# A decoder layer with routed experts on one core: routing each token tile beside the out projection instead of after it

## The reference

```python
x = x + merged @ w_out[l]
h2 = rms_norm(x, norm2_g[l])
...
gl = hf @ w_gr + b_gr                      # 4 groups
g_idx = argmax(gl); p_g = softmax(gl)[g_idx]
el = hf @ w_er + b_er                      # 4 x 8 experts
top_v, top_i = top_k(el[g_idx], 2)
w = softmax(top_v) * p_g
# each token goes through its 2 experts: (silu(h w_gate) * (h w_up)) w_down, weighted by w and added to x
```

## Time and profile before

| | us |
|---|---|
| median of 3 runs (lowest, highest) | 1543.49 (1543.43, 1547.29) |
| the profiled execution, its own time | 1544.72 |
| its span, first to last instruction | 1542.8 |
| TensorE busy in the span | 1428.2 (93%) |
| VectorE, ScalarE, GpSimd busy | 987.5, 790.1, 380.5 |
| mean granted TensorE clock | 0.965 of full speed |

### The profile page before, as it was taken

One profiled execution on the slowest core, in us unless ns is written; L12 is line 12 of the kernel. 1 busy time (PEld: TensorE's weight loads), 2 busy tenths in 40 slices (PEclk: granted clock), 3 DMA queues, 4 the chain that ended last, 5 costly groups with the idle time before them and its releaser, 6 DMA issues.

```text
span 1542.8 us, 20443 instructions
## 1 busy us (share of the span) xinstructions
PE 1428.2 (93%) x7251; PEld 1204.1 (78%) x7252; DVE 987.5 (64%) x1333; ACT 790.1 (51%) x1090; POOL 380.5 (25%) x497
## 2 busy tenths in 40 slices
PE   4899999999999999999999928999999999999980
PEld 4788888888888788888888827888888888888860
DVE  5664664664674532434332275988998898998865
ACT  5553453453453322323221235778787888887750
POOL 5324424424434200000000011223323323222310
PEclk9999999999999999999999859999999999999995
DMA  5210210210210334433152318999999999999958
GB/s 161 59 42 1 59 42 1 59 42 1 59 42 1 82 90 115 137 103 103 41 189 109 133 44 294 373 379 387 383 382 383 390 384 386 386 379 380 383 211 329
DMA packets 132130, 290.18 MB, mean 188 GB/s; under 512 B 15968, under 2 KB 94944, under 8 KB 107488
## 3 DMA queue, kind: packets, MB, share of 16 engines
q1 hardware_dynamic: 121696, 268.31, 48.4%
q0 software_dynamic: 9216, 16.80, 3.0%
q10 hardware_dynamic: 1152, 4.19, 0.7%
HBM read 280.87 MB, written 25.17 MB: 198 GB/s over the span
## 4 chain that ended last, share of the span: by engine, by line
PE 88%; DVE 3%; DMA 2%; POOL 2%; ACT 1%; issue 1%; SPq 0%; POOLq 0%; DVEq 0%; ACTq 0%
PE proj L87 17%; PE proj L89 17%; PE proj L88 17%; PE scores L87 7%; PE scores L89 7%; PE scores L88 7%; PE scores L665 2%; PE outs L729 2%; PE scores L545 2%; DMA comb<-y_rows 1%; PE turned L87 1%; PE turned L89 1%; PE turned L88 1%; PE outs L806 1%; PE turned L545 1%
## 5 line engine op out<-in xcount | busy, mean ns | idle before, releaser
L1642 DVE TENSOR_TENSOR w_low<-w_slot,w_high 128x2048 fp32r<-128x2048 f32 x192 | 438.3, 2290 | 68.4 <-ACT w_high L1078 67.4
L1078 ACT ACTIVATE w_high<-w_slot 128x2048 fp32r<-128x2048 f32 x192 | 367.0, 1918 | 120.4 <-DMA w_slot<-in_w_gate 63.8
L87 PE MATMUL proj<-w_high,xeH 128*128 128x512 f32 x512 | 203.8, 398 | 3.1 <-DVE xeL L1663 3.1
L89 PE MATMUL proj<-w_high,xeL 128*128 128x512 f32 x512 | 200.9, 392 | 0.0
L88 PE MATMUL proj<-w_low,xeH 128*128 128x512 f32 x512 | 200.4, 391 | 0.0
L913 ACT ACTIVATE wCH<-wC_in 128x1024 fp32r<-128x1024 f32 x48 | 47.6, 1052 | 155.7 <-DMA wC_in<-in_w_branch_b 155.7
L1321 DVE TENSOR_TENSOR wCL<-wC_in,wCH 128x1024 fp32r<-128x1024 f32 x48 | 56.9, 1236 | 92.2 <-ACT wCH L913 92.2
L87 PEld LDWEIGHTS proj<-w_high,xeH 128*128 128x128 f32 x512 | 97.1, 190 | 23.1 <-DVE xeL L1663 2.8
L89 PEld LDWEIGHTS proj<-w_high,xeL 128*128 128x128 f32 x512 | 96.8, 189 | 21.0
L88 PEld LDWEIGHTS proj<-w_low,xeH 128*128 128x128 f32 x512 | 97.0, 189 | 19.5
L87 PE MATMUL proj<-wBH,hTH 128*128 128x512 f32 x256 | 111.5, 436 | 0.0
(11 more groups left out here) (283 smaller groups left out, 3139.8 us busy)
## 6 DMA issues: line engine op xcount, KB each, us to landing
w_slot<-in_w_gate SPq DMA_DIRECT2D x64, 1024.0 KB
w_slot<-in_w_up SPq DMA_DIRECT2D x64, 1024.0 KB, 8.4
w_slot<-in_w_down SPq DMA_DIRECT2D x64, 1024.0 KB, 8.3
wC_in<-in_w_in SPq DMA_DIRECT2D x32, 512.0 KB, 5.0
wB_in<-in_w_in SPq DMA_DIRECT2D x16, 512.0 KB, 6.3
comb<-y_rows SPq DMA_DIRECT2D x16, 512.0 KB, 9.8
wA_in<-in_w_in SPq DMA_DIRECT2D x12, 512.0 KB, 6.3
x_all<-in_x SPq DMA_DIRECT2D x4, 1024.0 KB, 8.1
```

Of the source, the lines that this page charges most:

```text
L87: pe.matmul(out, lh, rh, start=start, stop=False)
L89: return pe.matmul(out, ll, rh, start=False, stop=stop)
L1078: act.activation(w_high[c][:], w_in6[c][:], ACT.Copy).then_inc(S["gu_high" if c < 4 else "d_high"], 1)
L1642: dve.tensor_tensor(w_low[c][:], w_in6[c][:], w_high[c][:].bitcast(F32), ALU.subtract).then_inc(S["gu_low" if c < 4 else "d_low"], 1)
```

## The change

Routing is done tile by tile, in the out projection's own time:

- TensorE's order has one loop of 16 halves, cnt = 8n + i. Between the products of half cnt stand the transposes of the residual x2's half before it (turn_half, not normalised) and the router product of that half (route_half), accumulated over the two halves by VectorE. The router's weights are multiplied by norm2_g first (wrg, GpSimd, from a new load g2_cols of norm2_g by columns), and the logits of a tile by its rstd afterwards.
- VectorE does a tile's routing in the steps top_group, two_experts (MAX and MAX_INDEX give the two best of 32) and place_rows; TensorE makes the tile's positions (positions_of) and adds its token numbers into one bank (rows_of).
- ScalarE squares by halves, copies the turned halves and scales h2; GpSimd multiplies h2 by norm2_g. Slots 0 and 1 of the first expert are loaded after half 0 and their w_high and w_low made in tiles 1 and 2 of half 1; slot 2 is loaded after the last out product, slot 3 after the last store of h2, slots 4 and 5 after the first gather.
- GpSimd gathers the first three experts from ids_gather directly, without the copy. The first expert's rows are transposed, and their high and low parts made, in two halves; its gate product waits for the first half only.
- The routing weights (gexp, vexp, wsel) are made after the row numbers. Several semaphores are merged.

```diff
+            sp.dma_start(g2_cols[:], T["norm2_g"][0].rearrange("(k p) -> p k", p=P),
+                         allow_slow_non_contiguous=True).then_inc(S["router_in"], DMA)
...
+            load_gu(0, (0, 1))
...
             sp.wait_ge(S["d_done"], 16)
-            load_gu(0, (0, 1))
+            load_gu(0, (2,))
+            store_h2(N_TILES - 1)
+            load_gu(0, (3,))
+            sp.wait_ge(S["xe_landed"], DMA)
...
+            def turn_half(cnt):
...
+                pe.wait_ge(S["x2_done"], cnt + 1)
...
+                for j in range(4):
+                    last = pe.transpose(bank(cnt % 2)[:, j * 128:(j + 1) * 128],
+                                        x2[:, i, n * 512 + j * 128:n * 512 + (j + 1) * 128], ident)
+                last.then_inc(S["x2T_done"], 1)
+            def route_half(cnt):
...
+                if cnt == 0:
+                    pe.wait_ge(S["wrg_done"], 1)
+                pe.wait_ge(S["x2T_out"], cnt + 1)
+                if n == 1:
+                    pe.wait_ge(S["logit_done"], cnt - 7)
+                for j in range(4):
+                    last = pe.matmul(OB[:, 36 * i:36 * i + 36], x2T[:, cnt % 2, j, :], wrg[:, 4 * n + j, :],
+                                     start=(j == 0), stop=(j == 3))
+                last.then_inc(S["lg_done"], 1)
+            def positions_of(t):
+                if t == 0:
+                    pe.wait_ge(S["masks_out"], 1)
+                else:
+                    pe.wait_ge(S["place_step"], 3 * t - 2)
+                pe.wait_ge(S["before_done"], 2 * t + 1)
+                last = pe.matmul(bank(2)[:, 0:32], count_masks[:, 0:128], mask[:, t, :], start=True, stop=(t == 0))
+                if t:
+                    last = pe.matmul(bank(2)[:, 0:32], count_masks[:, 128:256], before[:, t, :], start=False, stop=True)
+                last.then_inc(S["pos_mm"], 1)
+            def rows_of(t):
+                pe.wait_ge(S["place_step"], 3 * t + 3)
+                for c in range(2):
+                    last = pe.matmul(bank(3)[:, 0:32], pick[:, t % 2, c, :], keyid1[:, t, c, :],
+                                     start=(t == 0 and c == 0), stop=(t == 7 and c == 1))
+                last.then_inc(S["rows_mm"], 1)
+            for cnt in range(16):
+                out_proj(cnt, range(0, 2))
+                if cnt >= 1:
+                    turn_half(cnt - 1)
+                out_proj(cnt, range(2, 5))
+                if cnt >= 1:
+                    route_half(cnt - 1)
+                if cnt >= 10:
+                    positions_of(cnt - 10)
+                out_proj(cnt, range(5, 8))
+                if cnt >= 11:
+                    rows_of(cnt - 11)
+            turn_half(15)
+            route_half(15)
+            positions_of(6)
+            rows_of(5)
+            positions_of(7)
+            rows_of(6)
+            rows_of(7)
...
+            for half, done in ((0, "x0_T"), (1, "xeT_done")):
+                for k in range(4 * half, 4 * half + 4):
+                    last = pe.transpose(SC[:, 0, k * 128:(k + 1) * 128], xe[:, DS(k, 128, step=8)], ident)
+                last.then_inc(S[done], 1)
+            for c in range(4):
+                pe.wait_ge(S["gu_low"], c + 1)
+                if c == 0:
+                    pe.wait_ge(S["x0_L"], 1)
+                if c == 2:
+                    pe.wait_ge(S["xeL_done"], 1)
+                gate_up(pe, c).then_inc(S["w_free_gu"], 1)
...
+            for cnt in range(16):
+                square_half(cnt)
+                turned_half(cnt)
...
+                if cnt in (9, 10):
+                    high(w_high[cnt - 9][:], w_in6[cnt - 9][:], S[f"w_land{cnt - 9}"], DMA, S["gu_high"])
+                if cnt >= 8:
+                    i = cnt - 8
+                    act.wait_ge(S["n2_rstd"], 2 * i + 3)
...
+                    act.activation(h2[:, i % 2, :], x2[:, i, :], ACT.Copy, scale=rstd2[:, i:i + 1]).then_inc(S["h2_scaled"], 1)
...
+            for c in (2, 3):
                 high_slot(c, DMA)
-            x_high(1)
+            act.wait_ge(S["route_step"], R_DIFFS)
+            act.activation(gexp[:], gdiff[:], ACT.Exp).then_inc(S["weight_exps"], 1)
+            act.activation(vexp[:], vdiff[:], ACT.Exp).then_inc(S["weight_exps"], 1)
...
+            pool.wait_ge(S["router_in"], 5 * DMA)
+            pool.tensor_tensor(wrg[:], wr[:], g2_cols[:].unsqueeze(2).to_broadcast([P, N_KD, 36]), ALU.mult).then_inc(S["wrg_done"], 1)
...
+                pool.tensor_tensor(ms2[:, 1, i:i + 1], ms2[:, 0, i:i + 1], ssq[:, 1, i:i + 1], ALU.add).then_inc(S["n2_rstd"], 1)
...
+                pool.tensor_tensor(rstd2[:, i:i + 1], ms2[:, 1, i:i + 1], mhalf[:, 0:1], ALU.pow).then_inc(S["n2_rstd"], 1)
+                pool.wait_ge(S["h2_scaled"], i + 1)
+                pool.tensor_tensor(h2[:, i % 2, :], h2[:, i % 2, :], g2_row[:], ALU.mult).then_inc(S["h2_done"], 1)
...
+            def top_group(t):
...
+                dve.tensor_tensor(logits[:, t, :], OB[:, 36 * t:36 * t + 36], logits[:, t, :], ALU.add).then_inc(S["logit_done"], 1)
+                dve.wait_ge(S["logit_done"], t + 2)
+                dve.wait_ge(S["n2_rstd"], 2 * t + 3)
+                route(dve.scalar_tensor_tensor(logits[:, t, :], logits[:, t, :], rstd2[:, t:t + 1], br[:], ALU.mult, ALU.add))
+                gl = logits[:, t, 0:4]
+                route(dve.tensor_reduce(gmax[:, t:t + 1], gl, AX_X, ALU.max))
+                route(dve.scalar_tensor_tensor(gsc[:], gl, gmax[:, t:t + 1], const("rev_grp"), ALU.is_ge, ALU.mult))
+                route(dve.tensor_reduce(gtop[:], gsc[:], AX_X, ALU.max))
+                route(dve.tensor_scalar(gneg[:], gsc[:], gtop[:, 0:1], BIG_NEG, ALU.is_lt, ALU.mult))
+                route(dve.tensor_tensor(el[:], logits[:, t, 4:36].rearrange("p (g e) -> p g e", g=4),
+                                      gneg[:].unsqueeze(2).to_broadcast([P, 4, 8]), ALU.add))
+            def two_experts(t):
...
+                route(dve.max(vtop[:, t, :], el32))
+                route(dve.max_index(itop[:], vtop[:, t, :], el32))
+                route(dve.tensor_copy(eidx[:, t, :], itop[:, 0:2]))
+                route(dve.tensor_tensor(oh[:, t, :, :], iota32, eidx[:, t, :].unsqueeze(2).to_broadcast([P, 2, 32]), ALU.is_equal))
+                route(dve.tensor_tensor(mask[:, t, :], oh[:, t, 0, :], oh[:, t, 1, :], ALU.add))
...
+                    dve.tensor_tensor(before[:, t + 1, :], before[:, t, :].bitcast(F32), mask[:, t, :].bitcast(F32), ALU.add
...
+                dve.tensor_tensor(keyid1[:, t, :, :], oh[:, t, :, :], const("token_m")[:, t:16:8].unsqueeze(2).to_broadcast([P, 2, 32]),
...
+            def place_rows(t):
...
+                place(dve.tensor_tensor(posm[:], oh[:, t, :, :], bank(2)[:, 0:32].unsqueeze(1).to_broadcast([P, 2, 32]), ALU.mult))
+                place(dve.tensor_reduce(pos[:, t, :], posm[:], AX_X, ALU.add))
...
+                place(dve.tensor_tensor(pick[:, t % 2, :, :], iota128, pos[:, t, :].unsqueeze(2).to_broadcast([P, 2, 128]),
+                                        ALU.is_equal))
+            for i in range(N_TILES):
+                if i >= 1:
+                    top_group(i - 1)
+                add_residual(1, i)
...
+                if i >= 1:
+                    two_experts(i - 1)
...
+                    place_rows(i - 2)
+                if i in (1, 2):
+                    low(w_low[i - 1][:], w_in6[i - 1][:], w_high[i - 1][:], S["gu_high"], i, S["gu_low"])
+            top_group(7)
+            two_experts(7)
+            place_rows(6)
+            place_rows(7)
```

More of the change, by code:

```diff
@@ new lines, in _ @@
+            route(dve.tensor_tensor(gdiff[:], logits[:, :, 0:4], gmax[:].unsqueeze(2).to_broadcast([P, 8, 4]), ALU.subtract))
+            route(dve.tensor_tensor(vdiff[:], vtop[:, :, 1], vtop[:, :, 0], ALU.subtract))
+            dve.wait_ge(S["rows_mm"], 9)
+            route(dve.tensor_copy(counts_f[:, 0:32], bank(2)[:, 0:32]))
+            route(dve.tensor_reduce(counts_f[:, 32:33], counts_f[:, 0:32], AX_X, ALU.max))
+            dve.tensor_copy(counts_i[:], counts_f[:]).then_inc(S["tables_done"], 1)
@@ L1673, in hid_low @@
                                   hidH[:].rearrange("p a b -> p (a b)").bitcast(F32), ALU.subtract).then_inc(S["hidL_done"], 1)
-            for c in (1, 2):
-                low_slot(c, c + 1)
-            x_low(1)
+            low_slot(2, 3)
+            for half, ready, done in ((0, "x0_H", "x0_L"), (1, "xeH_done", "xeL_done")):
+                dve.wait_ge(S[ready], 1)
+                dve.tensor_tensor(xeL[:, 4 * half:4 * half + 4, :].rearrange("p a b -> p (a b)"), bank(half),
+                                  xeH[:, 4 * half:4 * half + 4, :].rearrange("p a b -> p (a b)").bitcast(F32), ALU.subtract
+                                  ).then_inc(S[done], 1)
             low_slot(3, 4)
```

495 lines of the change are left out of this document (216 added, 279 removed).

## The result

| | before | after |
|---|---|---|
| median of 20 runs each, us | 1545.02 | 1548.18 |
| lowest, highest | 1540.67, 1548.62 | 1544.39, 1551.29 |
| span of the profiled execution | 1542.8 | 1545.7 |
| mean granted TensorE clock | 0.965 | 0.969 |

The account below looks back on a forecast made before the run. TensorE was taken as the bound in out projection and experts, with a 47.7 us hole between, so an earlier first gate product ends the kernel earlier. +11.3 +14.0 +3.0 +5.0 -28.0 = +5.3 on 1543.5: 1549; range 1539 to 1556.

Parts of the forecast that it names:

- work put into the out projection: Router products, transposes, position and row-number products among the out products lengthen TensorE's stage: +11.3 us (10 to 12).
- wait for the router's weights: In the second out product TensorE stands from 781.1 to 795.1 for wrg, its inputs queued behind x: +14.0 us (12.5 to 18).
- half clock behind it: After TensorE's 14 us stand for wrg, some 6 us at half speed: +3.0 us lost (0 to 6).
- VectorE and GpSimd, tiles with w_low: Second half: GpSimd's h2 product holds VectorE up, making residuals 2.5 us late in two tiles: +5.0 us (1.2 to 8).
- the tail: From last out product to first gate product: 47.7 us shrinks to 19.7 (17.7 to 22 in all), -28.0.
- The 1.3 us for the new load: Part of the wait for wrg: g2_cols's 1024 small pieces ahead in SP's queue cost 1.3 us (0.5 to 4.8).
- the second rival: VectorE and GpSimd don't hold each other up: second half loses 1.2, tail about 2 less; 1543, no change; chance 0.24.
- the third: Rival: VectorE bounds the second half, stands there cost clock, or the gather waits for h2's rows or slot 3; 1554; 0.18.
- the copy and the 0.9 behind it go: Before the first gather, GpSimd's copy and the 0.9 us after it were claimed to disappear.
- The first rival: Router's inputs land in time, wrg made before 781.1: wait and its half clock go; 1532, faster; chance 0.08.

Follow-up runs that it names:

- all four edits: Changed kernel plus early router inputs, late count_masks, h2 made on VectorE, low parts of slots 0 and 1 over four tiles: 1524.4 us, 0.9864 of the kernel before.

## Why the prediction was right

The mechanism and the sign were right, and the time lies in the stated range. The size was half right: +5.3 was forecast and +2.9 measured, which is no change by the prediction's own 0.3%, to which it gave 0.42 against 0.46 for slower. That 1549 is so near 1548.2 is partly luck, since the kernel before came out at 1545.0 in 20 runs against 1543.5 in the first three. By its steps, all from the stage's start to the first gate product:

| step | predicted | measured |
|---|---|---|
| work put into the out projection | +11.3 | +9.8 |
| wait for the router's weights | +14.0 | +11.4 |
| half clock behind it | +3.0 | +3.45 |
| VectorE and GpSimd, tiles with w_low | +5.0 | +5.6 (0.5 of it half clock) |
| the tail | -28.0 | -27.5 |
| sum | +5.3 | +2.8 |

The first is what is left of 131.46 when the three below are taken off, less 101.15; the run with all four edits, which has no stands (110.5), has 9.3.

- **The work.** A half of the first eight takes 6.86 us (four from 812.43 to 839.85 in the residuals' starts: 27.42), so transposes and router product cost 1.41 and not 1.49, and a tile's positions and row numbers 0.35 more (7.2). All in all 1.5 us too high.
- **The wait** was named with its place, cause and start (TensorE stopped at 780.8, 781.1 predicted), and is the term that was mis-sized: 11.4 instead of 14.0. The 1.3 us for the new load aren't seen in the run without it in the queue. (The working was off too: half of 3.16 is 1.6.) The rest is the last bias going out at 786.56, 0.7 us sooner after x's first issue than before, GpSimd's product at 0.67 instead of 0.8, and a hand-over to TensorE of 0.06 instead of 0.2. The 0.7 are no more than scatter: the stand was 11.2 to 12.9 us in the other executions with the same queue.
- **The clock** was right in size, and that it comes from the standing is shown by the run that kept TensorE busy.
- **The two engines** were right in mechanism (shown by the run without GpSimd's product) and in size. With 2.37 us for 1024 columns the 2.3 ns a column held, and the late residuals were 2.4 and 2.9 us late against 2.5 twice. So the second rival (no holding up) is out. Of the third, two pieces came true: VectorE is full in two tiles, which the forecast had counted, and a stand of 2.5 us did bring a stretch at 0.50. It cost 0.5 us here, not 1.7 to 3, since the next residual was late anyway. In the run with g2_cols out of the queue the stretch came behind the second stand, and the residual after it 8.71 us behind its forerunner instead of 7.41: 1.3 us.
- **The tail** was right to 0.5 us with two errors that cancel in part. GpSimd's product held VectorE until 6.23 us after the last out product (6.2 predicted), and the row numbers were ready at 11.9 (12.0). But "the copy and the 0.9 behind it go" was wrong: the gather was issued 1.0 us after the row numbers without any copy (914.65 to 915.66; the trace puts this wait down to counts_i, but the kernel waits for ids_gather alone), as it was issued 0.85 after the copy in the earlier trace rows. That time belongs to the gather. And the gather took 4.56 us from its issue, not 5.1. Neither h2's last store nor slot 3 came late. Another 0.4 us is VectorE's step gneg, 0.67 us instead of 0.23, while GpSimd filled xe with zeros (908.87 to 909.82); the prediction had no such term. Of what the Trainium skill (SBUF — State Buffer, Who interferes with whom) infers on descriptors this case shows the same as before: the first gather, while VectorE stood still, was issued in 1.31 us, against 2.41 beside w_low.
- **The first rival** was worked out wrongly, though it had little chance. Had the router's inputs been in time, the kernel would have taken 1542 and not 1532, since a second wait stood right behind the first: the constants on ScalarE. The prediction asked what is queued in front of GpSimd, and not what is queued in front of the copy on ScalarE. With both waits gone it is 1533.5, so 1532 was near for that.

## What to carry to other kernels

When a step is moved forward to lie beside other work, its inputs move forward too: list every load that it reads, on every engine that takes part, and find each one's place in the queue. Here two such loads stood behind 4 MB and hid each other; together they cost 15 us in a change that came out 2.9 us slower. And work that was given to GpSimd to relieve VectorE relieved nothing here, where both had two operands in SBUF: it cost VectorE 10.8 us of waiting in place of 10.3 us of work. Look for what VectorE has to do between the issue of GpSimd's instruction and its end, and count the overlap as lost.

## What the runs showed of the hardware that was not expected

- VectorE and GpSimd, both with two operands in SBUF, took turns by whole instructions: the one issued second ended with or after the first (GpSimd's product 3.46 us instead of 2.37 beside w_low, VectorE's step 2.15 instead of 0.26 beside the product), while VectorE's step that reads PSUM (860.21) took 0.19, and in the tail the reduction between logits and gsc, with one operand, 0.17. The Trainium skill (SBUF — State Buffer, Who interferes with whom) says that the pair of ports that the two share is locked for a whole instruction, and that a VectorE instruction with two inputs in SBUF contends with GpSimd's reads where one with a single such input, outside its two-port modes, does not; this case agrees, by the 2.15 and the 0.17.
- MAX of 32 columns took 0.18 us and MAX_INDEX two instructions, 0.09 and 0.18: as cheap as any small step.
- In the tail VectorE's gneg on 128x4 took 0.67 us beside GpSimd's filling of xe with zeros, which reads nothing, in the changed kernel (909.17 beside 908.87 to 909.82, so it ended with the filling) and in six other runs. It took 0.23 where the two don't meet, as with h2 on VectorE, or where it began only 0.16 us ahead of the filling's end.
- Products that nobody reads kept TensorE's clock at 1.00 across the stand of 11 us and across one of the tail's two holes in each of the two runs that filled them. In the other hole it fell in spite of them: to 0.52 in 915 to 918 in one run, to 0.63 in 886 to 889 in the other. In the trace that brought back the 3.45 us of the stand. In the tail it brought nothing in the timed runs, but there the filling also outlasted its hole, by 0.7 us once and by 1.3 the other time.
